# Hybrid decoder step on Trainium2: projections reordered around the score products of the gated recurrence, Pool's products given to ScalarE and VectorE

## The chip, the core and the metric

One NeuronCore of a Trainium2 chip runs the whole program. The metric is the device time of one execution in microseconds (us), median of the runs. The engines are TensorE (PE in the profile; its weight loads are PEld), VectorE (DVE), ScalarE (ACT), GpSimd (POOL) and the sync engine SP, which here only issues transfers.

## What is computed

A single decoder layer for 256 prompt tokens, 16 meta tokens ahead of them and 8 samples of one token each, width 1024, all in float32. From the reference, cut:

```python
u = _rmsnorm(tok, norm_mix[l]) @ w_in[l]          # 7 groups of 512 columns
bg, cg, hv, q, fx, iv, og = jnp.split(u, SPLIT_POINTS, axis=-1)
y_conv = cg * conv3(bg * hv)                      # causal, width 3
f = lb + (1 - lb) * jax.nn.sigmoid(fx); kk = 1 - f
b = jnp.cumsum(log f)                             # per head, 4 heads of 128
scores = einsum('bhtk,bhsk,bhtsk->bhts', q, k, exp(b_t - b_s), causal)
o = scores @ v + (q * jnp.exp(b)) @ S0
S_new = exp(b_last) * S0 + (k * exp(b_last - b)).T @ v
y_rec = per_head_rmsnorm(o) * rec_gain * silu(og)
h = h + concat(y_conv, y_rec) @ w_out
# then: rmsnorm, top-4-of-32 experts (1024 -> 2 x 1024 -> 1024, clamped
# SwiGLU, biases), residual add, final rmsnorm
```

The states of the recurrence and of the convolution are outputs too. The 32 experts' weights are 403 MB of the 431 MB that a run moves.

## The kernel before

**Columns and tiles.** The normalised tokens stand transposed in `xT3` (128 x 8 x 280: 24 columns for samples and meta tokens, then 256 prompt columns). A projection group is 2 MB of weights. Three helpers of the TensorE program use it: `columns_of` (L1280) gives one head's or one quarter's 128 output rows by 280 tokens, eight float32 products; `rows_of` (L1264) gives a tile of 128 tokens by 512 columns, eight products of 512; `stacked` (L1272) does the small tile with 32 narrow products.

**Stage 1** runs forget gate `FX`, value `IV`, query `QG`, output gate `OG`, in this order, each whole, from about 16.5 to 84 us. ScalarE and VectorE make meanwhile from `FX` the gate `f`, its logarithm, the running sums, and the decays, and copy the value and the query out of PSUM.

**Stage 2** is the list `SCHEDULE`, built from `PROJ` (the remaining twelve column groups: `BG` and `HV` by turns, then `CG`) and from `PIECES`, two or three pieces after each group. All engines walk the same list and take from it what is theirs. The pieces: `khat` turns the decayed keys into token rows; `score` is one of 16 score products; `outer` makes the samples' outer products and VectorE adds them to the scaled old states `s0`; `state` and `recur` are the prompt's state and output products, `os` those of the samples.

**Scores.** Each chunk of 128 tokens has a diagonal product and seven levels. For level l the tokens are cut into blocks of 2^l; keys of the earlier block and queries of the later one are scaled by the decay to the border between them. VectorE makes the difference (`diff`, L859), ScalarE two exponentials (`exps`, L611), VectorE the scaled operand (`weigh`, L869), TensorE four products of it with itself (L1342), and VectorE takes from the 128x128 result, by a mask, the part that is this level's (L951). There are two such operands and two PSUM banks (2 and 3) in use by turns, so a product waits for the operand that VectorE made two scores earlier in the list, and for the masked copy before that.

**Pool** makes `vdiag`, the samples' values spread over a diagonal, scales `s0` by the gate (L510, four instructions), and afterwards loads the expert biases and splits them into three bfloat16 parts (L514 to L521).

**Queues.** SP issues the weights in the order of a list and waits for the event that frees each place: the weights and the scratch tiles lie in a ring of eight slots of 2 MB that the expert weights use later. The loads of expert 0 go out one by one in stages 2 and 3: after the output gate, after `HV`, after `CG`, after the samples' states are stored, and in the output projection; a further one then goes out whenever TensorE gives a slot back.

**Stage 3** from 168.6 us: output projection (L1397), router, the choice of the experts, the first gather. **Stage 4** from 219.6 us: 16 pairs of experts, 12 loads of 2 MB a pair. A pair gathers its tokens by one-hot products of bfloat16 parts (L1531, 72 products: 8 column tiles, 3 token tiles, 3 parts), multiplies with the two weight matrices (L1590, L1635), and adds the rows back.

```python
1326                if what == "score":
...
1340                    for h in range(HEADS):
1341                        at = slice(h * P, (h + 1) * P)
1342                        last = mm(ps[:, 2 + a % 2, at], left[:, at], right[:, at], start=True, stop=True)
```

## Time and profile before

| | before |
|---|---|
| median of 3 runs, us | 1161.08 (1159.2 to 1161.52) |
| profiled execution, its own time | 1161.72 |
| span of the profile | 1160.0 |
| TensorE busy | 1062.0 (92%) |
| VectorE, ScalarE, Pool busy | 287.3, 168.3, 48.6 |
| DMA over the span | 431.46 MB, 372 GB/s |
| mean granted clock | 0.987 |
| chain that ended last | PE 61%, DMA 32%, DVE 3%, ACT 2% |

The span is what the trace covers; the profiled execution took 1.7 us more than it, and 0.64 more than the median. Busy shares are averages over four stages; the order of the instructions in time, the waits and the chain that ended last tell what limits each.

### The profile page before, as it was taken

Reading aid. Unit: us, or ns where it says so; the run is one execution under the profiler, and the core shown is the slowest. Engines: PE = TensorE matmul, PEld = TensorE weight load, DVE = VectorE, ACT = ScalarE, POOL = GpSimd, SP = SyncE. Lnnn points to the kernel's source line nnn. Section 1 sums busy time; section 2 is a strip of 40 time slices with the busy share of each in tenths; the row PEclk is TensorE's granted clock in tenths of the full one; section 3 lists DMA queues with packets and bytes.
Section 4 is the critical chain, followed back from the end, with each engine's and each line's share of the span. In section 5 each row is a group of like instructions: output and inputs, shape, how many; then the busy total and the mean of one; then the engine's idle time right before and its main releaser. Section 6 shows DMA issues by size and latency. Waiting matters only on the chain.

```text
span 1160.0 us, 13518 instructions
## 1 busy us (share of the span) xinstructions
PE 1062.0 (92%) x5617; PEld 485.9 (42%) x5617; DVE 287.3 (25%) x513; ACT 168.3 (15%) x381; POOL 48.6 (4%) x71
## 2 busy tenths in 40 slices
PE   6998899899999999899989998999898989898986
PEld 5666764443434343434343434343434343434322
DVE  3447742630202020202020202020202020202023
ACT  3311103310101010101010101010101010101012
POOL 3260012000000000000000000000000000000000
PEclk9999999899999999999999999999999999999998
DMA  9860238399999999999999999999999999999991
GB/s 335 292 241 4 99 147 314 112 409 429 428 425 429 427 429 427 428 430 426 431 427 427 431 426 431 427 428 430 426 431 427 429 429 427 431 425 429 427 429 76
DMA packets 47842, 431.46 MB, mean 372 GB/s; under 512 B 4942, under 2 KB 13686, under 8 KB 23136
## 3 DMA queue, kind: packets, MB, share of 16 engines
q1 hardware_dynamic: 45760, 428.23, 88.4%
q0 software_dynamic: 752, 2.56, 0.7%
q8 instruction: 23, 0.38, 0.1%
q10 hardware_dynamic: 1296, 0.20, 0.1%
q14 instruction: 11, 0.09, 0.0%
HBM read 427.50 MB, written 3.48 MB: 372 GB/s over the span
## 4 chain that ended last, share of the span: by engine, by line
PE 61%; DMA 32%; DVE 3%; ACT 2%; issue 2%; SPq 1%; ACTq 0%; DVEq 0%
DMA ring<-in_expert_w 31%; PE ps L1635 19%; PE ps L1590 17%; PE ps L1286 7%; PE ps L1531 5%; PE ps L1268 2%; PE ps L1397 2%; PE ps L1548 2%; ACT mem L722 2%; PE ps L1624 2%; PE ps L1342 1%; DMA ring<-in_meta_tokens 0%; SPq L387 0%; PE ps L1260 0%; PE ps L1276 0%
## 5 line engine op out<-in xcount | busy, mean ns | idle before, releaser
L1590 PE MATMUL ps<-ring,mem 128*64 128x512 f32 x2048 | 459.2, 596 | 42.4 <-DMA ring<-in_expert_w 41.9
L1590 PEld LDWEIGHTS ps<-ring,mem 128*64 128x64 f32 x2048 | 155.1, 137 | 335.8 <-issue 334.8
L1635 PE MATMUL ps<-ring,mem 128*64 128x512 f32 x1024 | 225.2, 597 | 5.3 <-ACT mem L738 3.0
L1117 DVE TENSOR_TENSOR mem<-mem,ps 128x1024 f32<-128x1024 f32 x32 | 39.1, 1222 | 463.6 <-PE ps L1548 463.6
L1635 PEld LDWEIGHTS ps<-ring,mem 128*64 128x64 f32 x1024 | 86.0, 138 | 133.6 <-issue 133.6
L731 ACT ACTIVATE mem<-mem 128x512 f32<-128x512 f32 x32 | 20.2, 630 | 569.0 <-DVE mem L1179 569.0
L1286 PE MATMUL ps<-mem,ring 128*128 128x280 f32 x320 | 82.7, 417 | 1.0 <-DVE mem L933 0.6
L1548 PE MATMUL ps<-mem 128*128 128x512 f32 (+3 forms) x192 | 80.0, 610 | 0.0
L1286 PEld LDWEIGHTS ps<-mem,ring 128*128 128x128 f32 x320 | 62.6, 200 | 18.7 <-issue 2.8
L1531 PEld LDWEIGHTS ps<-mem 128*128 128x128 bf16 x1080 | 60.3, 98 | 12.2 <-issue 12.2
L1531 PE MATMUL ps<-mem 128*128 128x128 bf16 x1080 | 62.9, 219 | 0.0
L1179 DVE TENSOR_SCALAR mem<-ps 128x512 f32<-128x512 f32 x32 | 22.1, 692 | 146.4 <-PE ps L1590 146.4
L751 ACT ACTIVATE mem<-ps 128x512 f32<-128x512 f32 x32 | 19.1, 597 | 209.2 <-PE ps L1635 209.2
L1548 PEld LDWEIGHTS ps<-mem 128*128 128x128 f32 (+3 forms) x192 | 23.3, 154 | 54.3 <-issue 54.3
L1121 DVE TENSOR_TENSOR mem<-mem,ps 8x512 f32<-8x512 f32 x16 | 10.8, 675 | 118.6 <-PE ps L1548 118.6
L722 ACT ACTIVATE mem<-ps,mem 128x128 f32<-128x128 f32 x124 | 35.3, 368 | 27.2 <-PE ps L1531 24.3
L1624 PE MATMUL ps<-mem 128*128 128x128 f32 x128 | 20.3, 304 | 16.5 <-ACT mem L722 13.7
L1397 PE MATMUL ps<-ring,mem 128*128 128x512 f32 x64 | 28.9, 600 | 0.2 <-DVE mem L933 0.2
L1268 PE MATMUL ps<-ring,mem 128*128 128x512 f32 x64 | 27.8, 592 | 0.0
L1624 PEld LDWEIGHTS ps<-mem 128*128 128x128 f32 x128 | 17.1, 210 | 17.9 <-issue 12.1
L1342 PE MATMUL ps<-ring 128*128 128x128 f32 x112 | 16.6, 300 | 8.2 <-DVE ring L875 8.2
L1181 DVE TENSOR_SCALAR mem<-ps 128x512 f32<-128x512 f32 x32 | 21.8, 681 | 0.0
(268 smaller groups left out, 521.0 us busy)
## 6 DMA issues: line engine op xcount, KB each, us to landing
ring<-in_expert_w SPq DMA_DIRECT2D x192, 2048.0 KB, 26.8
ring<-in_w_in SPq DMA_DIRECT2D x7, 2048.0 KB, 20.6
ring<-in_w_out SPq DMA_DIRECT2D x2, 2048.0 KB, 10.1
ring<-in_state_rec SPq DMA_DIRECT2D x4, 512.0 KB, 10.5
out<-ring SPq DMA_DIRECT2D x4, 512.0 KB, 11.0
out<-mem SPq DMA_DIRECT2D x5, 256.0 KB, 5.2
ring<-in_x_prompt SPq DMA_DIRECT2D x2, 512.0 KB, 4.4
mem<-in_x_prompt POOLq DMA_DIRECT2D x2, 512.0 KB, 4.1
```

The lines of the kernel that those rows point to most:

```text
L722: last = act.activation(xgT4[:, k, 4 * half + q], ps[:, 6 + half, q * P:(q + 1) * P], ACT.Copy, scale=gffn_q[:, 4 * half + q:4 * half + q ...
L1117: dve.tensor_tensor(h3[:, m], h3[:, m], ps[:, 4 + 2 * m:6 + 2 * m, :].rearrange("p a n -> p (a n)"), ALU.add)\
L1179: dve.tensor_scalar(glu[:, at], psA[:, half * D:(half + 1) * D:2], LIMIT, None, ALU.min)\
L1268: last = mm(ps[:, bank, :], xT3[:, t, at:at + P], w_sb[g][:, t, :], start=(t == 0), stop=(t == KT - 1))
L1286: last = mm(ps[:, bank, 0:TOK], w_sb[g][:, t, j * P:(j + 1) * P], xT3[:, t, :], start=(t == 0), stop=(t == KT - 1))
L1342: last = mm(ps[:, 2 + a % 2, at], left[:, at], right[:, at], start=True, stop=True)
L1397: last = mm(ps[:, (6, 4)[i] + n, :], yT3[:, k, TILE_COL[i]:TILE_COL[i] + P], wout_sb[k // 4][:, t, n * 512:(n + 1) * 512], start=(k == 0), ...
L1531: last = mm(out, hn_hi_mid_lo[m][:, part, part_cols(t)], oh5[:, k, m].rearrange("p e s -> p (e s)"), start=(m == 0 and part == 0), stop=(m ...
L1548: last = mm(to, left[:, m * P:m * P + r], right[:, half * HALF:(half + 1) * HALF], start=True, stop=True)
L1590: done = mm(ps[CAP * e:CAP * e + CAP, b, :], xgT4[:, k, t, CAP * e:CAP * e + CAP], ring[:, slot[e], col:col + HALF], start=False, stop=(t ...
L1624: done = pe.transpose(ps[:, 6 + half, q * P:(q + 1) * P], lin[:, half * HALF + q:(half + 1) * HALF:4], ident)
L1635: done = mm(ps[CAP * e:CAP * e + CAP, 4 + half, :], actT3[:, 4 * v + t, CAP * e:CAP * e + CAP], ring[:, slot[e], col:col + HALF], start=(v ...
```

## The change

* **Order of the stages.** Query weights are loaded second, and TensorE projects `FX`, then `QG` (into banks 0, 1, 4, 7 at once, one for each head). `IV` and `OG` move into `SCHEDULE`, in halves of four products of 512 (`rows_of` has a parameter `half`) or as the small stacked tile, with one score product after each. The `BG`, `HV` and `CG` groups follow, also mostly with one score between two groups.
* **Half-width products.** A level's product streams only the later blocks' columns, 64 instead of 128 a head, and the masked copy handles 256 elements instead of 512. The diagonal product stays.
* **Pool's work.** `vdiag` and the scaling of `s0` become eight ScalarE copies with a scale each (five times eight in all); the bias split becomes three ScalarE copies and two VectorE subtractions. Pool asks for the biases after the first forget group. The clearing of `b1_raw` is gone.
* **Gathers.** The sample tile's products use 8 rows instead of 128, in the first gather and in every pair.
* The gate arithmetic (sigmoid times value, L889 to L891) and the scaled queries `qhat` stand in the schedule instead of ahead of it.

```diff
-        PIECES = [("khat", 0)] + [("score", s) for s in range(3)] + [("outer", 0)] + ...
-        PROJ = [(g, j) for j in range(4) for g in (BG, HV)] + [(CG, j) for j in range(4)]
+        Q_BANKS = [0, 1, 4, 7]
+        SCHEDULE = [("rows", (IV, 0, 0))] + DIAG[0] + [("rows", (IV, 0, 1))] + level(0)
+        SCHEDULE += [("rows", (IV, 1, 0)), ("khat", 0)] + level(1) + [("rows", (IV, 1, 1))] + level(2)
+        SCHEDULE += [("b1", 0), ("rows", (IV, 2, 0)), ("vdiag", 0)] + level(3) + [("rows", (OG, 0, 0)), ("s0", 0)] + level(4)
+        SCHEDULE += [("rows", (OG, 0, 1)), ("s0", 1)] + level(5) + [("rows", (OG, 1, 0)), ("s0", 2)] + level(6)
...
+        SCHEDULE += [("proj", (BG, 1)), ("outer", 1), ("proj", (HV, 1))] + level(9)
...
             sp.dma_start(w_sb[FX], w_group(FX)).then_inc(win_in[FX], 16)
+            sp.dma_start(w_sb[QG], w_group(QG)).then_inc(win_in[QG], 16)
             sp.dma_start(w_sb[IV], w_group(IV)).then_inc(win_in[IV], 16)
-            sp.dma_start(w_sb[QG], w_group(QG)).then_inc(win_in[QG], 16)
...
-            for h in range(HEADS):
-                pool.tensor_tensor(s0[:, h], s0[:, h], bcast(fS3[:, h].unsqueeze(2), [P, NS, P]), ALU.mult)\
-                    .then_inc(s0f_sb, 1)
-
+            pool.wait_ge(fx_ps, 1)
             for part in range(3):
                 pool.dma_start(b1_raw[32 * part:32 * part + 32, :], expert_b1[0]).then_inc(b1_in, 16)
...
+                if what == "s0":
+                    act.wait_ge(s0_in, 16 * HEADS)
+                    act.wait_ge(fS_sb, 1)
+                    for b in range(NS):
+                        last = act.activation(s0[:, a, b], s0[:, a, b], ACT.Copy, scale=fS3[:, a, b:b + 1])
+                    last.then_inc(s0f_sb, 1)
...
+                if what == "b1":
+                    dve.wait_ge(b1_step, 4)
+                    dve.tensor_tensor(b1_parts[64:96, :], b1_raw[64:96, :], b1_parts[64:96, :], ALU.subtract)\
+                        .then_inc(b1_sb, 1)
...
+                    else:
+                        pe.wait_ge(sog_sb, bank - 4)
                     columns_of(g, j, bank, done)
...
-                        left = right = wl3[:, n % 2]
+                        left = wl3[:, n % 2]
+                        later = cut(left, 2 << STEPS[n][1])[:, :, 1 << STEPS[n][1]:]
...
+                            last = mm(ps[:, 2 + a % 2, h * 64:(h + 1) * 64], left[:, at],
+                                      later[:, h * m:(h + 1) * m], start=True, stop=True)
...
-                            last = mm(out, hn_hi_mid_lo[m][:, part, part_cols(t)],
-                                      oh5[:, k, m].rearrange("p e s -> p (e s)"),
+                            r = [P, P, NS][m]
+                            last = mm(out, hn_hi_mid_lo[m][0:r, part, part_cols(t)],
+                                      oh5[0:r, k, m].rearrange("p e s -> p (e s)"),
```

**Where the instructions stand.** TensorE before, from the second half of stage 1 into the schedule (L1268 and L1276 are `rows_of` and `stacked`, L1286 `columns_of`, L1323 and L1326 the khat turns, L1342 the score products, L1352 the outer products):

```order
L1286 MATMUL ps<-mem,ring 128x280 x32
L1268 MATMUL ps<-ring,mem 128x512 x16
L1276 MATMUL ps<-ring,mem 32x128 x32
L1286 MATMUL ps<-mem,ring 128x280 x8
L1323 MATMUL ps<-mem 128x128 x8
L1326 MATMUL ps<-mem 128x128
L1342 MATMUL ps<-mem 128x128 x4
L1286 MATMUL ps<-mem,ring 128x280 x8
L1342 MATMUL ps<-ring 128x128 x8
L1352 MATMUL ps<-ring,mem 128x512 x3
L1286 MATMUL ps<-mem,ring 128x280 x8
```

TensorE of the change, behind forget gate and query (L1289, L1298 are now the rows and the stacked tile, L1308 the column groups, L1367 the diagonal score, L1370 a level's score, L1347 and L1349 the khat turns):

```order
L1308 MATMUL ps<-mem,ring 128x280 x64
L1289 MATMUL ps<-ring,mem 128x512 x4
L1367 MATMUL ps<-mem 128x128 x4
L1289 MATMUL ps<-ring,mem 128x512 x4
L1370 MATMUL ps<-ring 128x64 x4
L1289 MATMUL ps<-ring,mem 128x512 x4
L1347 MATMUL ps<-mem 128x128 x8
L1349 MATMUL ps<-mem 128x128
L1370 MATMUL ps<-ring 128x64 x4
L1289 MATMUL ps<-ring,mem 128x512 x4
L1370 MATMUL ps<-ring 128x64 x4
L1298 MATMUL ps<-ring,mem 32x128 x32
```

The scores moved ahead of most of the value and gate rows, which now stand between them; a level's products have 64 columns.

ScalarE of the change, around the fourth to the sixth level (L629 copies the value, L644 is the bias copy, L649 vdiag, L616 the exponentials of the levels, L655 the scaling of `s0`, L635 the gate's exponential):

```order
L616 ACTIVATE ring<-ring 128x16x16 x2
L644 ACTIVATE mem<-mem 32x2048
L629 ACTIVATE mem<-ps 128x128
L649 ACTIVATE ring<-mem 128x128 x8
L616 ACTIVATE ring<-ring 128x8x32 x2
L655 ACTIVATE ring<-ring,mem 128x128 x8
L616 ACTIVATE ring<-ring 128x4x64 x2
L635 ACTIVATE mem<-ps 128x512
L655 ACTIVATE ring<-ring,mem 128x128 x8
L616 ACTIVATE ring<-ring 128x256 x2
```

Groups of eight small products that Pool did in one instruction now stand between the exponentials of the levels.

VectorE of the change, from the bias subtraction to the first gate (L914 the subtraction, L879 `diff`, L888 `weigh`, L972 the masked copy, L909 to L911 the gate):

```order
L914 TENSOR_TENSOR mem<-mem 32x2048
L879 TENSOR_TENSOR ring<-mem 128x512
L888 TENSOR_TENSOR ring<-ring,mem 128x16x16 x2
L972 COPY_PREDICATED ring<-mem,ps 128x32x8
...
L972 COPY_PREDICATED ring<-mem,ps 128x4x64
L909 TENSOR_SCALAR mem<-mem 128x512
L910 RECIPROCAL mem<-mem 128x512
L911 TENSOR_TENSOR mem<-mem,ps 128x512
```

The subtraction stands ahead of a level's preparation, and the gates stand between the masked copies instead of ahead of all scores.

## Rows read from the trace of the kernel before

**Rows 1.** The chain that ended last: start us, us, what.
```profile
253.35 4.14 PE ps L1531 x72
...
275.12 7.02 PE ps L1590 x32
...
329.74 7.02 PE ps L1590 x32
...
939.47 7.09 PE ps L1590 x32
...
998.21 7.09 PE ps L1590 x32
```

**Rows 2.** A window of the expert stage: busy by engine, clock, DMA share, GB/s.
```profile
234.00:239.00 5.00, 5.00 (x23) 1.59 (x23) 1.22 (x1) 0.00 (x0) 0.00 (x0) 1.00 0.99 423
```

**Rows 3.** Timeline of TensorE, stage 1: start us, us, line, instructions.
```profile
33.64 13.90 PE L1268 MATMUL ps<-ring,mem 128*128 128x512 f32 x32
47.46 1.95 PE L1276 MATMUL ps<-ring,mem 128*32 128x128 f32 x64
49.35 15.36 PE L1286 MATMUL ps<-mem,ring 128*128 128x280 f32 x64
64.55 13.90 PE L1268 MATMUL ps<-ring,mem 128*128 128x512 f32 x32
...
80.26 4.04 PE L1286 MATMUL ps<-mem,ring 128*128 128x280 f32 x16
```

**Rows 4.** Timeline of TensorE, stage 2 (two records a float32 product).
```profile
84.13 1.04 PE L1323 MATMUL ps<-mem 128*128 128x128 f32 x8
...
101.55 1.95 PE L1342 MATMUL ps<-ring 128*128 128x128 f32 x16
103.33 3.94 PE L1286 MATMUL ps<-mem,ring 128*128 128x280 f32 x16
...
108.09 1.13 PE L1352 MATMUL ps<-ring,mem 32*128 32x512 f32 x6
...
140.53 3.92 PE L1342 MATMUL ps<-ring 128*128 128x128 f32 x16 [3.10 <-DVE ring L875]
...
155.60 1.94 PE L1380 MATMUL ps<-ring,mem 128*32 128x512 f32 x16
...
168.60 13.97 PE L1397 MATMUL ps<-ring,mem 128*128 128x512 f32 x32 [0.24 <-DVE mem L933]
```

**Rows 5.** Waits (us in total, times, longest), and a window of stage 2.
```profile
PE ps L1342 <- DVE ring L875: 8.2, 4, 3.1
...
142.00:144.00 2.00, 2.00 (x10) 1.91 (x10) 1.65 (x4) 0.40 (x3) 0.00 (x0) 0.50 1.04 442
```

**Rows 6.** Weight loads and products by line: durations in ns, or busy and mean.
```profile
L1342 PEld LDWEIGHTS ps<-ring x112: 186/192/338, 89.8 to 151.5; 128*128 128x128 f32 x112
...
L1276 PEld LDWEIGHTS ps<-ring,mem 128*32 128x32 f32 x128 | 3.4, 110 | 1.5 <-issue 1.5
...
195.47 0.67 PE L1437 MATMUL ps<-mem 8*128 8x8 f32 x8
...
L1531 PE MATMUL ps<-mem x1080: 219/219/230, 253.3 to 1069.1; 128*128 128x128 bf16 x180
```

**Rows 7.** Timeline of ScalarE, then of VectorE.
```profile
41.42 1.11 ACT L607 ACTIVATE mem<-mem 128x1088 f32<-128x1088 f32 x1 [2.59 <-DVE mem L856]
...
218.19 1.14 ACT L722 ACTIVATE mem<-ps,mem 128x128 f32<-128x128 f32 x4 [2.90 <-PE ps L1496]
...
79.57 3.35 DVE L890 RECIPROCAL mem<-mem 128x512 f32<-128x512 f32 x1
...
113.19 0.70 DVE L866 TENSOR_TENSOR ring<-mem 128x512 f32<-128x512 f32 x1
113.79 0.77 DVE L875 TENSOR_TENSOR ring<-ring,mem 128x256 f32<-128x256 f32 x2
114.46 0.73 DVE L951 COPY_PREDICATED ring<-mem,ps 128x512 f32<-128x512 uint32 x1
```

More of the change, by code:

```diff
@@ L643, in _ @@
                     act.activation(ctmp, ps[:, 5, 0:TOK], ACT.Copy).then_inc(bg_sb, 1)
+                if what == "b1":
+                    act.activation(b1_parts[32:64, :], b1_raw[32:64, :], ACT.Copy).then_inc(b1_step, 1)
+                if what == "vdiag":
+                    act.wait_ge(own_sb, 1)
+                    act.wait_ge(v_sb, 3)
+                    for b in range(NS):
+                        last = act.activation(vdiag[:, b * P:(b + 1) * P], vtok3[:, 2, 0:P], ACT.Copy, scale=own[:, b:b + 1])
+                    last.then_inc(vdiag_sb, 1)
+                if what == "s0":
+                    act.wait_ge(s0_in, 16 * HEADS)
+                    act.wait_ge(fS_sb, 1)
+                    for b in range(NS):
+                        last = act.activation(s0[:, a, b], s0[:, a, b], ACT.Copy, scale=fS3[:, a, b:b + 1])
+                    last.then_inc(s0f_sb, 1)
                 if what == "khat":
@@ L899, in _ @@
             dve.wait_ge(q_sb, HEADS)
-            for c in range(2):
-                dve.wait_ge(decay_exp, c + 2)
-                link(dve.tensor_copy(decay_all[:, 4 * c:4 * c + 4],
-                                     qhat3[:, c].rearrange("p (h t) -> p h t", h=HEADS)[:, :, P - 1]))
-                dve.tensor_tensor(qhat3[:, c], qhat3[:, c], qC3[:, c], ALU.mult).then_inc(qhat_sb, 1)
             weigh(0)
             for what, a in SCHEDULE:
+                if what == "gate":
+                    g = sog3[:, a] if a < 2 else sogS
+                    dve.wait_ge(og_exp, a + 1)
+                    link(dve.tensor_scalar(g, g, 1.0, None, ALU.add))
+                    link(dve.reciprocal(g, g))
+                    dve.tensor_tensor(g, g, ps[:, 5 + a, 0:WIDE[a]], ALU.mult).then_inc(sog_sb, 1)
@@ L1262, in _, with rows_of @@
                         last.then_inc(xT_ps, 1)
-            def rows_of(g, i, bank, done):
+            def rows_of(g, i, half, bank, done):
                 at = TILE_COL[i]
-                for t in range(KT):
+                for t in range(4 * half, 4 * half + 4):
                     last = mm(ps[:, bank, :], xT3[:, t, at:at + P], w_sb[g][:, t, :],
                               start=(t == 0), stop=(t == KT - 1))
-                last.then_inc(done, 1)
+                if half:
+                    last.then_inc(done, 1)
             def stacked(g, bank, done):
@@ L1293, in _ @@
                 columns_of(FX, h, 2 + h % 2, fx_ps, first=(h == 0))
-            pe.wait_ge(win_in[IV], 16)
-            for i in range(2):
-                rows_of(IV, i, 5 + i, iv_ps)
-            stacked(IV, 7, iv_ps)
             for h in range(HEADS):
-                if h >= 2:
-                    pe.wait_ge(q_sb, h - 1)
-                columns_of(QG, h, h % 2, q_ps)
-            pe.wait_ge(win_in[OG], 16)
-            pe.wait_ge(fx_exp, HEADS)
-            for i in range(2):
-                rows_of(OG, i, 2 + i, og_ps)
-            stacked(OG, 4, og_ps)
-            pe.wait_ge(v_sb, 3)
-            for what, a in SCHEDULE:
+                columns_of(QG, h, Q_BANKS[h], q_ps)
+            for what, a in SCHEDULE:
+                if what == "rows":
+                    g, i, half = a
+                    if half == 0:
+                        pe.wait_ge(win_in[g], 16)
+                        if g == OG:
+                            pe.wait_ge(v_sb, i + 1)
+                        elif i == 2:
+                            pe.wait_ge(q_sb, HEADS)
+                    done = iv_ps if g == IV else og_ps
+                    if i < 2:
+                        rows_of(g, i, half, 5 + i, done)
+                    else:
+                        stacked(g, 7, done)
                 if what == "proj":
@@ L1329, in _ @@
                     if a < 2:
[L1330 removed]
+                        pe.wait_ge(fx_exp, HEADS)
                     else:
@@ L1495, in gather_first @@
                 for t in steps:
-                    last = mm(ps[:, 6 + t // 4, (t % 4) * P:(t % 4 + 1) * P], hn_hi_mid_lo[m][:, part, part_cols(t)],
-                              oh5[:, 0, m].rearrange("p e s -> p (e s)"), start=(m == 2 and part == 0 and t % 4 == 0),
+                    r = [P, P, NS][m]
+                    last = mm(ps[:, 6 + t // 4, (t % 4) * P:(t % 4 + 1) * P], hn_hi_mid_lo[m][0:r, part, part_cols(t)],
+                              oh5[0:r, 0, m].rearrange("p e s -> p (e s)"), start=(m == 2 and part == 0 and t % 4 == 0),
                               stop=(m == 1 and part == 2 and t % 4 == 3))
```

113 lines of the change are left out of this document (60 added, 53 removed).

## The prediction

> **What bounds the kernel now.** I read the chain that ended last first. The pairs of experts follow each other at a fixed pace there: early in the run the same step comes back after 329.74 - 275.12 = 54.6 us, late in the run after 998.21 - 939.47 = 58.7 us [rows 1]. A late period is twelve loads of 2.1 MB, 25.2 MB in 58.7 us, or 429 GB/s; the window at 234 us, one and a half periods after the expert stage began, already shows the DMA engines 0.99 busy at 423 GB/s [rows 2]. So the early pairs run at TensorE's pace on a ring of eight full slots, the late ones at the transfers' pace, and the transfers are busy without a break from the moment when the first slots are given back. The end is therefore that moment plus a fixed amount of bytes. It moves one for one with the time at which TensorE enters the expert stage, and nothing that is saved inside a pair of experts (4.1 us of slack in each late pair) moves it.
>
> Next I looked at what stands before that stage, on TensorE alone, in order of time. From 33.64 to 80.26 us it has no gap: value rows 13.82 us, the stacked small tile 1.89, four query column groups 64.55 - 49.35 = 15.2 (3.80 each), output gate rows like the value rows [rows 3]. From 80.26 us to the start of the output projection at 168.60 the picture is another: a score of four products takes (103.33 - 101.55)/2 = 0.89 us when nothing is in the way, while two scores together took 3.92 us at 140.53 [rows 4]. The waits view says why: four waits of scores for the scaled operand that VectorE makes (the function weigh), 8.2 us in all, the longest 3.1, and behind the long one the granted clock is 0.50, the lower of its two levels, 1.2 GHz [rows 5].
>
> **What TensorE's work there is without waits.** Twelve column groups of 3.80 = 45.6; sixteen scores of 0.89 = 14.2; the khat turns 1.2 (eight in 1.04, and a ninth); three rounds of outer products of 1.1 = 3.3; the state products, twelve at a score's rate of 0.223 = 2.7; two recur steps, sixteen products each of the same kind over both = 3.6; the sample products 1.9 [rows 3, 4]. Sum 72.5 us. It took until about 167.8 (0.8 before 168.60, in which the small turns stand), that is 87.5 from 80.26. So **15.0 us are lost** there, 8.2 as the waits above, the rest as smaller waits and work at half clock.
>
> **The change, part by part.**
> (1) *Order.* The query moves up behind the forget gate, and its operands are ready at about 33.6 + 15.2 = 48.8 us, where before the scores began at 84. The value and gate rows (31.4 us, now in eight halves of 3.46 and two stacked tiles) and the twelve column groups stand between the scores, one piece of some 3.5 to 7.6 us between two scores. A score's preparation on VectorE is 0.70 + 0.77 + 0.73 = 2.2 us, plus an exponential on ScalarE [rows 7]. It fits into each gap. Before, pairs and triples of scores stood back to back with 0.9 us in between, and that is what could not be covered. If no wait is left, the output projection's start is 33.64 + 46.6 (80.26 - 33.64, same rows and groups) + 72.5 + 0.8 = 153.5 instead of 168.60: **-15.1 us**.
> (2) *Which waits come closest.* I walked the new order with the durations above. ScalarE now has five groups of eight small products (vdiag and four s0), each group 8 x 0.285 = 2.3 us (four 128x128 with a scale in 1.14 [rows 7]), and three bias copies of 2048 columns, about 1.9 to 2.2 each by the 1.11 us for 1088. VectorE has two bias subtractions of 2048 columns, 2.4 each by 0.60 for 512 (113.79 - 113.19), and three gates of which two cost 3.35 for the reciprocal plus 1.1. The subtraction in the schedule ends at about 72.2, the operand for the fifth level (level 4) at 73.5, and TensorE reaches that score at 73.7: slack 0.2. The second gate ends at 95.4, and TensorE wants its bank for the first HV group at 95.3: a tie. Everywhere else the slack is some 0.9 us or more. The bias rows are asked for on Pool's queue after the first forget group, at about 33.6 - 3 x 3.8 = 22.2, and ScalarE wants them before its decay exponential, which ran at 41.42 [rows 7]; were they late, the query copies behind them on ScalarE would be late too. They are 0.8 MB beside full transfers, and the nearest row is only the 2 MB at 423 GB/s, so 2 to 10 us; I take them as in time. For the two ties and the handshakes I take off 0.6: **+0.6**, with 0 and 7.5 (half of today's loss) as ends.
> (3) *Half-width products.* Fourteen level scores stream 64 columns instead of 128, the weights stay 128 columns wide. A score is eight TensorE records, 0.111 each. Does the record get shorter? Its weight load takes 192 ns against 110 ns for 32 columns [rows 6]: 82 ns for 96 columns, 0.85 ns a column, 109 ns for 128. That is the whole record already, so the load bounds it and streaming less saves nothing. The other bound is the shortest record here with 128 weight columns, the 8-row turns at 0.67/8, at most 0.084, and less the tail, 0.59/8 = 0.074 [rows 6]; they are turns, a different kind, and would give 14 x 8 x (0.111 - 0.074) = 4.1 us. Pure streaming at half would give 14 x 8 x 0.055 = 6.2. I take **0**, and keep 6 as the far end. VectorE's masked copy gets shorter (256 columns), which only adds slack.
> By the Trainium skill ("TensorE: Matmul & The Clock Gate", section on LDWEIGHTS) the load time grows with the columns of the weights alone, 128 of them in 107 ns, and its section on the back-to-back issue gap gives a matmul of up to 64 columns some 60 cycles; by the first the sum keeps its 0 here, by the second it would be the 6 us of pure streaming. The measured slope is on the side of the first.
> (4) *Pool relieved.* Its products and bias arithmetic lay beside TensorE's gapless stretch and nothing in the chain waited for them: 0. Covered now by the rows that TensorE does meanwhile; without that cover it is item 2's price.
> (5) *Eight-row gathers.* The sample tile's gather products (24 of 72 a pair) run with 8 rows. Inside the pairs they cannot help (slack above), in the first gather they stand before a wait: 0.
> (6) *Queues.* Each load of SP waits for the same event as before. The first expert load waits for the output gate (80.3 before, 89.5 now, wanted only in the expert stage), the others for the HV and CG groups, the stores, and the output projection, which all move with TensorE. 0. The second output weight waits for the value rows (about 69 now) and is wanted only in the second half of the output projection.
>
> Sum: 15.1 - 0.6 = **14.5 us** less. The profiled execution took 1161.72 us (span 1160.0) and so becomes 1147.2; it lies 0.64 above the median of 1161.08, from which I get **1146.6 us**. About 0.2% (2.3 us) is what a measurement tells from no change.
>
> **Rivals.**
> *The half width pays* (against: the slope of the loads; for: turns with short streams do run at 0.074). 4 to 6 us more: 1140.5 to 1142.5. The skill's section on the issue gap, named above, is the rule that would bring this about.
> *A new wait on ScalarE or VectorE takes the place of the old.* ScalarE is strictly in order: 2.3 us of s0 products stand before an exponential, and the bias arithmetic before the fifth operand. If these forty products took 0.4 instead of 0.285, the ScalarE chain is 4.6 us longer between 70 and 90 us, the gates and exponentials slip, and each wait near 3 us brings a stretch of half clock behind it, as at 140 us. Half of today's loss would remain: 1154. For: two ties; against: all other slacks.
> *The eight-row gathers slow the pairs, and the run ends slower.* Today 72 gathers flow at 4.14/72 = 57 ns [rows 1], though each is 219 ns long by itself [rows 6]. If the change of the row count broke that overlap, 24 x 0.162 = 3.9 us a pair: just under the slack of 4.1, no loss. From 5.1 us a pair on (if the products before and behind are held up too), it costs more than 1 us in each of 15 pairs and cancels the gain; at 6 us it is 15 x 1.9 = 28 - 14.5, so 1175. Nothing in the profile speaks for it but that 128-row and 8-row products never stood side by side here.
> *The change doesn't do what it says*: the expert stage's start is held by something off TensorE, such as the last prefetched loads. Each of them is released by TensorE's own output projection, so I see little for it: 1160 to 1162.
>
> **How the numbers follow.** Forecast (1144 to 1149) 0.62; half width 0.13; new wait, 1150 to 1157, 0.17; gathers 0.04; no effect 0.04. Range: down to the half-width case, 1140.5, up to half of the loss kept, 1154; outside are the worst waits and the last two, some 0.12. Faster by over 0.2%: 0.62 + 0.13 + 0.17 = 0.92; within: 0.04; slower: 0.04.
>
> **What would show it.** In the new profile the output projection starts at 153 to 155; the scores' waits for the scaled operand fall from 8.2 to under 1.5 us; no window from 50 to 150 has a clock of 0.5; level scores still take about 0.89; a late pair takes 58.7 as before, and TensorE waits longer for the ring in all. I am wrong if the start of the output projection moves by 15 and the end doesn't, if scores take 0.5, or if a window between 65 and 100 shows TensorE idle for ScalarE.

## The result, and the profile after

| | before | after |
|---|---|---|
| median of the runs | 1161.3 us (1159.2 to 1161.8, 4 runs) | 1145.94 us (1145.66 to 1146.98, 4 runs) |
| span of the profiled execution | 1160.0 us | 1143.9 us |
| start of the output projection | 168.60 us | 152.07 us |
| first weight product of the experts | 219.57 us | 204.49 us |
| POOL busy | 48.6 us | 23.8 us |

The medians lie 15.4 us apart. The ratio of the runs is 0.9876 with a 95% interval of [0.9862, 0.989], that is 14.4 us less (12.8 to 16.0); the ratio is on record beside the medians and is not their quotient, here and below. The forecast was 1146.6 us. Three executions (1410.77 us in the run of the half width alone, 1424.49 in the bunched one, 2227.62 of the kernel before) were far slower than the rest and stand outside the ratios, but in the counts and medians given; without them those two medians are 1161.48 and 1151.35.

The timeline of TensorE in the kernel after, the answer to [rows 3] and [rows 4] (start us, us, line, instructions, idle time before and its releaser):

```profile
16.34 30.43 PE L1308 MATMUL ps<-mem,ring 128*128 128x280 f32 x128 [0.69 <-ACT mem L584]
46.61 3.60 PE L1289 MATMUL ps<-ring,mem 128*128 128x512 f32 x8
...
54.37 1.00 PE L1370 MATMUL ps<-ring 128*128 128x64 f32 x8
55.21 3.65 PE L1289 MATMUL ps<-ring,mem 128*128 128x512 f32 x8
...
91.99 1.14 PE L1381 MATMUL ps<-ring,mem 32*128 32x512 f32 x6
93.42 4.04 PE L1308 MATMUL ps<-mem,ring 128*128 128x280 f32 x16 [0.29 <-DVE mem L911]
...
152.07 13.11 PE L1428 MATMUL ps<-ring,mem 128*128 128x512 f32 x30 [0.24 <-DVE mem L951]
```

Between 46.61 and 152.07 TensorE has one idle time that shows, 0.29 us: the first HV group waits for the second gate, which is one of the two ties that the prediction named. The scores' waits for the weighed operand, 8.2 us in [rows 5], are gone, and no window of this stretch is below full clock. The stretch takes 105.46 us; the working of the prediction gives 105.3 for it (154.1, its start of the output projection with the 0.6 of item 2, less 48.8). A score takes 54.37 to 55.21, that is 0.84 us.

The pairs, by the chain (start us, us, what), for [rows 1], and the waits (total, times, longest):

```profile
238.28 5.69 PE ps L1564 x72
...
276.02 7.02 PE ps L1623 x32
...
571.78 7.09 PE ps L1623 x32
...
630.53 7.09 PE ps L1623 x32
...
689.27 7.09 PE ps L1623 x32
```

```profile
PE ps L1623 <- DMA ring<-in_expert_w: 13.9, 15, 1.6
```

The late pair takes 58.75 us as before, 4.14 us of gathers have become 5.69, and TensorE's wait for the ring of expert weights (the line above) fell from 41.9 us to 13.9. So something became dearer in the pairs, and it is hidden under the transfers.

### The profile page after: what moved, and what is told of

It reads as the page before. It is cut to its first block, busy times and chain, and to the rows that moved or that the text cites. A ratio compares the mean times of both kernels' runs of the same rounds, so it can differ in the third digit from the quotient of the medians.

```text
span 1143.9 us, 13559 instructions
## 1 busy us (share of the span) xinstructions
PE 1085.4 (95%) x5617; PEld 474.0 (41%) x5617; DVE 288.5 (25%) x515; ACT 185.3 (16%) x424; POOL 23.8 (2%) x60
## 4 chain that ended last, share of the span: by engine, by line
PE 71%; DMA 22%; ACT 2%; DVE 2%; issue 1%; SPq 0%; ACTq 0%; DVEq 0%
PE ps L1623 22%; DMA ring<-in_expert_w 22%; PE ps L1668 20%; PE ps L1564 7%; PE ps L1308 6%; PE ps L1581 3%; PE ps L1289 2%; PE ps L1428 2%; PE ps L1657 2%; ACT mem L735 2%; PE ps L1370 1%; PE ps L1528 1%; PE ps L1573 1%; DMA ring<-in_x_prompt 0%; PE ps L1281 0%
## 5 line engine op out<-in xcount | busy, mean ns | idle before, releaser
L1623 PE MATMUL ps<-ring,mem 128*64 128x512 f32 x2048 | 456.9, 596 | 14.4 <-DMA ring<-in_expert_w 13.9
L1623 PEld LDWEIGHTS ps<-ring,mem 128*64 128x64 f32 x2048 | 145.4, 137 | 313.6 <-issue 312.6
L1668 PE MATMUL ps<-ring,mem 128*64 128x512 f32 x1024 | 232.3, 613 | 4.6 <-ACT mem L751 2.6
L1668 PEld LDWEIGHTS ps<-ring,mem 128*64 128x64 f32 x1024 | 86.0, 141 | 140.4 <-issue 140.4
L1564 PE MATMUL ps<-mem 128*128 128x128 bf16 (+1 forms) x1080 | 86.2, 220 | 0.0
L1308 PE MATMUL ps<-mem,ring 128*128 128x280 f32 x320 | 78.4, 401 | 1.0 <-ACT mem L584 0.7
L1564 PEld LDWEIGHTS ps<-mem 128*128 128x128 bf16 (+1 forms) x1080 | 60.3, 96 | 35.5 <-issue 12.2
L1308 PEld LDWEIGHTS ps<-mem,ring 128*128 128x128 f32 x320 | 59.8, 190 | 17.7 <-issue 3.1
L1581 PEld LDWEIGHTS ps<-mem 128*128 128x128 f32 (+3 forms) x192 | 23.3, 154 | 54.3 <-issue 54.3
L1289 PE MATMUL ps<-ring,mem 128*128 128x512 f32 x64 | 29.1, 597 | 0.0
L1207 DVE SCALAR_TENSOR_TENSOR mem<-mem 128x512 f32<-128x512 f32 x32 | 20.7, 688 | 0.5
```

The source lines that it names most:

```text
L1289: last = mm(ps[:, bank, :], xT3[:, t, at:at + P], w_sb[g][:, t, :], start=(t == 0), stop=(t == KT - 1))
L1308: last = mm(ps[:, bank, 0:TOK], w_sb[g][:, t, j * P:(j + 1) * P], xT3[:, t, :], start=(t == 0), stop=(t == KT - 1))
L1564: last = mm(out, hn_hi_mid_lo[m][0:r, part, part_cols(t)], oh5[0:r, k, m].rearrange("p e s -> p (e s)"), start=(m == 0 and part == 0), sto ...
L1581: last = mm(to, left[:, m * P:m * P + r], right[:, half * HALF:(half + 1) * HALF], start=True, stop=True)
L1623: done = mm(ps[CAP * e:CAP * e + CAP, b, :], xgT4[:, k, t, CAP * e:CAP * e + CAP], ring[:, slot[e], col:col + HALF], start=False, stop=(t ...
L1668: done = mm(ps[CAP * e:CAP * e + CAP, 4 + half, :], actT3[:, 4 * v + t, CAP * e:CAP * e + CAP], ring[:, slot[e], col:col + HALF], start=(v ...
```

## Experiments

The theory by then: the order brings the gain, the work taken off GpSimd nothing, the half width nothing, the eight-row gathers nothing. The first four kernels take the change apart.

**Gathers back to 128 rows, the rest as after.** (`P` in place of `r` in the operands of the gathers, and the padding cleared on GpSimd.)

```diff
-                            r = [P, P, NS][m]
-                            last = mm(out, hn_hi_mid_lo[m][0:r, part, part_cols(t)],
-                                      oh5[0:r, k, m].rearrange("p e s -> p (e s)"),
+                            last = mm(out, hn_hi_mid_lo[m][:, part, part_cols(t)],
+                                      oh5[:, k, m].rearrange("p e s -> p (e s)"),
```

> The changed kernel, but the sample tile's gather products run with all 128 rows again (Pool clears the part of b1_raw behind the samples, as before the change). Theory: the eight-row products cost TensorE 1.55 us a pair (72 gathers took 5.69 instead of 4.14 us), which the transfers hide, and about 1.5 us in the first gather, which nothing hides, since the expert stage began 15.1 us earlier while the output projection began 16.5 us earlier. Then 72 gathers take 4.14 us again, the expert stage begins near 203.0 instead of 204.5, and the run takes about 1144.5 against 1145.9 of the changed kernel. Rival: the longer stretch at half clock in the first gather was chance; then the stage begins at 204.5 and the run takes 1145.9. Second rival: pairs are what bounds the end; then 15 x 1.55 = 23 us less, 1123.

Measured: 1145.66 us (1143.06 to 1147.14, 4 runs), ratio 0.9857 [0.9842, 0.9872]. Gathers 4.14 us, wait for the ring 40.3 us, and 50.95 us from the start of the output projection (153.88) to the first weight product, as the 50.97 of before; the kernel after needs 52.42. So the eight rows cost 1.55 us a pair, hidden, and about 1.5 us in the first gather, which is not hidden but too small to stand out in the whole time. The expert stage itself began at 204.83, not near the 203.0 that was expected, since everything up to the query's end came 1.8 us later in this execution; the section on why the prediction was right comes back to this.

**Scores back to full width, the rest as after.** (The masked copy runs over all columns too.)

```diff
-                        else:
-                            m = later.shape[1] // HEADS
-                            last = mm(ps[:, 2 + a % 2, h * 64:(h + 1) * 64], left[:, at],
-                                      later[:, h * m:(h + 1) * m], start=True, stop=True)
+                        last = mm(ps[:, 2 + a % 2, at], left[:, at], right[:, at], start=True, stop=True)
```

> The changed kernel with level scores of 128 columns a head and the masked copy over 512 elements, as before. Theory (the weight load bounds a short product): a level score goes from 0.84 back to 0.89 us, 14 x 0.05 = 0.7 us, so about 1146.6 against 1145.9. Rival (the stream bounds it): 4 to 6 us more, 1150 to 1152. A second rival: VectorE's longer masked copy uses up the small slacks and TensorE waits for the scaled operand, 1 to 3 us more.

Measured: 1146.93 us (1145.51 to 1148.55, 4 runs), ratio 0.9877 [0.9862, 0.9893]; from the query's end at 46.93 to the output projection at 152.52 it is 105.59 us, beside 105.46. The half width is worth nothing that can be measured here, and 0.13 us of the stretch.

**Eight-row gathers alone, in the kernel before** (the first diff the other way round).

> The kernel before, but the sample tile's gather products run with 8 rows. Theory: 72 gathers take 5.7 us instead of 4.14, an early pair 56.2 instead of 54.6, a late pair 58.7 as before, and the expert stage begins about 1.5 us later than 219.6 if the first gather's longer half clock comes from these products: about 1162.5 against 1161.1. Rival (chance): 1161.1. Rival of the prediction (pairs are held up and the end moves with them): 1184.

Measured: 1162.65 us (1159.67 to 1163.99, 11 runs), ratio 1.0012 [1.0003, 1.0021]. Gathers 5.69 us, early period 56.2 us in place of 54.6, wait for the ring 14.4 us in place of 41.9. One part of the change is a small loss.

**The order alone**: the new table, but full width, 128-row gathers, and GpSimd does the products of vdiag and S0 and the bias split as before. The core of the diff against the kernel before, cut:

```diff
-        PIECES = [("khat", 0)] + [("score", s) for s in range(3)] + [("outer", 0)] + [("score", s) for s in range(3, 6)]
...
+        SCHEDULE = [("rows", (IV, 0, 0))] + DIAG[0] + [("rows", (IV, 0, 1))] + level(0)
...
```

> The changed kernel with only its new order: scores of full width, Pool does vdiag, the scaling of s0 and the bias split, gathers of 128 rows. Theory: the order carries all of the gain; 1145.9 + 0.7 (full width) - 1.5 (first gather) = 1145.1. Rival: ScalarE's and VectorE's taking over of Pool's products carries a part of it, because Pool's results (ready near 80 us) hold the outer products or the scores; then 1147 to 1152. Second rival: half width carries it; then above 1150.

Measured: 1156.25 us (1155.01 to 1156.75, 5 runs), ratio 0.9953 [0.9939, 0.9966]. Here the theory falls: the order alone brings 4.4 us by the medians (1160.61 is the kernel before on that chip), 5.5 by the ratio, of some 15. The first rival names the right part, the work taken off GpSimd, but for another reason and with a smaller loss (1147 to 1152); the second, the half width, is ruled out by the kernel with full-width scores. Its timelines show where the rest went; first TensorE, then VectorE, then GpSimd:

```profile
92.41 1.13 PE L1368 MATMUL ps<-ring,mem 32*128 32x512 f32 x6
103.19 6.00 PE L1301 MATMUL ps<-mem,ring 128*128 128x280 f32 x16 [9.64 <-DVE mem L911]
```

```profile
87.11 3.66 DVE L881 TENSOR_TENSOR ring<-mem 128x512 f32<-128x512 f32 x1
90.69 4.13 DVE L890 TENSOR_TENSOR ring<-ring,mem 128x256 f32<-128x256 f32 x2
94.75 0.71 DVE L965 COPY_PREDICATED ring<-mem,ps 128x512 f32<-128x512 uint32 x1
95.36 3.66 DVE L909 TENSOR_SCALAR mem<-mem 128x512 f32<-128x512 f32 x1
99.05 3.35 DVE L910 RECIPROCAL mem<-mem 128x512 f32<-128x512 f32 x1
```

```profile
86.14 4.08 POOL L525 TENSOR_TENSOR mem<-mem 96x2048 f32<-96x2048 f32 x1
90.28 2.23 POOL L526 CAST mem<-mem 32x2048 bf16<-32x2048 f32 x1
92.56 1.99 POOL L527 CAST mem<-mem 32x2048 bf16<-32x2048 f32 x1
94.63 4.11 POOL L528 TENSOR_TENSOR mem<-mem 32x2048 bf16<-32x2048 f32 x1
```

The two halves of a row of weighing (one row of the profile with x2) take 0.75 us together by themselves and 4.13 here; the add in front of the gate's reciprocal takes 0.42 and here 3.66. The stretched ones end 0.3 to 0.6 us behind an instruction of GpSimd (90.77 against 90.22, 94.82 against 94.55, 99.02 against 98.74), while the masked copy and the reciprocal run at their usual length beside it. The second gate is 9.8 us late (103.13 beside 93.36 in the kernel after), TensorE idles 9.64 us and has a group at half clock behind it (6.00 for 4.04). That is 11.3 us to the output projection (163.80 beside 152.52 of the full-width kernel). In the kernel before, the same GpSimd instructions ran from 49.8 to 80.9 us, where VectorE had little to do. Even there it was not free, though: the profiled execution of the kernel before was only spared by 0.07 us. Its second gate's add began just ahead of GpSimd's last instruction, a clearing (start us, us):

```profile
79.11 0.43 DVE L889 TENSOR_SCALAR mem<-mem 128x512 f32<-128x512 f32 x1 [1.78 <-ACT mem L632]
79.18 1.67 POOL L521 MEMSET mem<- 128x1536 f32 x1
```

```profile
86.45 0.33 PE L1329 MATMUL ps<-mem 128*128 128x128 f32 x1 [1.14 <-DVE mem L891]
```

The last line is from the kernel before with half width, further below. There the add began at 79.25, behind the clearing at 79.18, took 1.59 us, and TensorE waited 1.14 us for the gates. The kernel before with eight-row gathers and the one with doubled gathers, whose instructions are those of the kernel before up to there, show the same (adds of 1.60 and 1.65 us, waits of 1.15 and 1.20). So which of the two begins first, by less than 0.1 us, is worth about 1.2 us in the old order. Where the add came first, the clearing took 1.67 us for 1.38.

New theory: GpSimd's work holds up VectorE's instructions of certain kinds for its whole length, and this costs where VectorE is next on TensorE's path. Four kernels tell which instructions, and whether the spacing of the scores matters beside it.

**GpSimd does vdiag and S0 only.** Added on GpSimd, taken from ScalarE:

```diff
+            pool.tensor_tensor(vdiag.rearrange("p (b v) -> p b v", b=NS),
+                               bcast(vtok3[:, 2, 0:P].unsqueeze(1), [P, NS, P]),
+                               bcast(own.unsqueeze(2), [P, NS, P]), ALU.mult).then_inc(vdiag_sb, 1)
...
+                pool.tensor_tensor(s0[:, h], s0[:, h], bcast(fS3[:, h].unsqueeze(2), [P, NS, P]), ALU.mult)\
+                    .then_inc(s0f_sb, 1)
```

> The kernel after, but GpSimd does the ones products of the values (vdiag) and the scaling of S0 again, as large two-operand instructions; the bias split stays on ScalarE and VectorE. Theory A (what GpSimd's work costs is that VectorE's own instructions stretch while it runs, 0.75 to 4.1 us each, and this reaches TensorE only where VectorE's work is next on TensorE's path): GpSimd's products fall at about 68 to 85 us, so VectorE's weighing and row work there stretches to 3 to 4 us an instruction as in e4, but the stretched scores are only a few us behind other projections: output projection start 152 to 155, time 1145.9 to 1149. Theory B (any two-operand work on GpSimd in the score stage costs as e4 did): output projection start about 160 to 164 and 1154 to 1156.

Measured: 1154.17 us (1152.31 to 1155.73, 6 runs), ratio 0.9949 [0.9932, 0.9967], output projection at 161.00. Time and start are those that theory B named, so the expectation missed. The rows show theory A's mechanism all the same; what failed is its price, since the cover that I had counted on was not there. From the query's end (48.90) to the output projection it is 112.10 us, 6.6 more than in the kernel after. First TensorE, then VectorE, then GpSimd:

```profile
70.05 3.65 PE L1289 MATMUL ps<-ring,mem 128*128 128x512 f32 x8
78.48 1.79 PE L1370 MATMUL ps<-ring 128*128 128x64 f32 x8 [4.77 <-DVE ring L888]
80.06 4.65 PE L1289 MATMUL ps<-ring,mem 128*128 128x512 f32 x8
```

```profile
69.68 2.28 DVE L914 TENSOR_TENSOR mem<-mem 32x2048 bf16<-32x2048 f32 x1 [1.89 <-ACT mem L656]
71.99 2.27 DVE L879 TENSOR_TENSOR ring<-mem 128x512 f32<-128x512 f32 x1
74.19 4.15 DVE L888 TENSOR_TENSOR ring<-ring,mem 128x256 f32<-128x256 f32 x2
```

```profile
70.03 3.69 POOL L514 TENSOR_TENSOR ring<-mem 128x1024 f32<-128x1024 f32 x1 [45.41 <-ACT mem L641]
73.68 8.71 POOL L521 TENSOR_TENSOR ring<-ring,mem 128x1024 f32<-128x1024 f32 x4
```

Here GpSimd is held up as well: its first product takes 3.69 us for 1.90, since VectorE's subtraction, begun 0.35 us before, runs to 71.96. Then each of VectorE's waits for one of GpSimd's (71.99 to 74.26 against 73.72). Whoever begins first keeps the other out for one whole instruction. The bias subtraction stands in front of the fifth level's operand, which was the other tie (in the kernel after that operand is ready at 71.05 and its score begins at 71.25), so TensorE idles 4.77 us.

**GpSimd does the bias split only**, begun when two groups of S0 are scaled.

```diff
+            pool.wait_ge(s0f_sb, 2)
...
+            link(pool.tensor_tensor(b1_raw[0:96, :], b1_raw[0:96, :], b1_parts[0:96, :], ALU.subtract))
...
-            dve.tensor_tensor(b1_raw[0:96, :], b1_raw[0:96, :], b1_parts[0:96, :], ALU.subtract).then_inc(b1_step, 1)
```

> The kernel after, but GpSimd splits the biases again (both subtractions and the copies), begun when two heads' groups of S0 are scaled, about 80 us; the products of vdiag and S0 stay on ScalarE. Theory A (the loss of e4 against the kernel after lies in the GpSimd instructions that run beside VectorE's second gate, at 86 to 99 us): the second gate ends some 5 to 10 us later, TensorE shows an idle stretch of 5 to 9 us ahead of the first state group near 93 us and a window at half clock behind it, output projection start 158 to 163, time 1151 to 1156. Theory B (the loss lay in the earlier products of vdiag and S0, or in the full width): start 152 to 153.5 and the time of the kernel after, 1145 to 1147.

Measured: 1154.11 us (1153.93 to 1155.19, 6 runs), ratio 0.9953 [0.9939, 0.9968], output projection at 160.86. Theory A is right: TensorE idles 6.43 us before the first HV group and that group takes 6.41 for 4.04. From the query's end (46.92) to the output projection it is 113.94 us, 8.5 more than in the kernel after. Which kinds are held up is best seen here, first VectorE, then GpSimd:

```profile
86.65 0.76 DVE L882 TENSOR_TENSOR ring<-mem 128x512 f32<-128x512 f32 x1
87.33 6.31 DVE L891 TENSOR_TENSOR ring<-ring,mem 128x256 f32<-128x256 f32 x2
93.57 0.71 DVE L969 COPY_PREDICATED ring<-mem,ps 128x256 f32<-128x256 uint32 x1
94.08 1.60 DVE L910 TENSOR_SCALAR mem<-mem 128x512 f32<-128x512 f32 x1
95.71 3.35 DVE L911 RECIPROCAL mem<-mem 128x512 f32<-128x512 f32 x1
99.10 0.69 DVE L912 TENSOR_TENSOR mem<-mem,ps 128x512 f32<-128x512 f32 x1
99.71 1.40 DVE L910 TENSOR_SCALAR mem<-mem 128x128 f32<-128x128 f32 x1
```

```profile
86.94 4.39 POOL L514 TENSOR_TENSOR mem<-mem 96x2048 f32<-96x2048 f32 x1
91.40 1.96 POOL L515 CAST mem<-mem 32x2048 bf16<-32x2048 f32 x1
93.40 1.99 POOL L516 CAST mem<-mem 32x2048 bf16<-32x2048 f32 x1
95.48 4.11 POOL L517 TENSOR_TENSOR mem<-mem 32x2048 bf16<-32x2048 f32 x1
99.64 1.38 POOL L518 MEMSET mem<- 128x1536 f32 x1
```

Held up: products with both operands in SBUF (6.31 for 0.75), and the scalar add from SBUF (1.60 for 0.45; the small one 1.40 for 0.22, behind a memset). Not held up: the masked copy and the gate's last product, which read one operand from PSUM, and the reciprocal. By the Trainium skill ("SBUF — State Buffer", section on who interferes with whom) GpSimd and VectorE share one pair of ports that is locked for a whole instruction; a vector instruction with two SBUF inputs contends for it with a GpSimd instruction that reads SBUF, and an operation with a scalar can contend when it runs in a two-port fast mode. These rows agree with it for the kinds that it names, the memset's row too: the add takes 0.42 us for the 512 columns that a product takes 0.68 for, so it may well run in such a mode, which no row shows directly. The reciprocal it does not name.

**The spacing.** The scores of levels 3 to 5 back to back, the rest as after:

```diff
-        SCHEDULE += [("b1", 0), ("rows", (IV, 2, 0)), ("vdiag", 0)] + level(3) + [("rows", (OG, 0, 0)), ("s0", 0)] + level(4)
-        SCHEDULE += [("rows", (OG, 0, 1)), ("s0", 1)] + level(5) + [("rows", (OG, 1, 0)), ("s0", 2)] + level(6)
+        SCHEDULE += [("b1", 0), ("rows", (IV, 2, 0)), ("vdiag", 0), ("rows", (OG, 0, 0)), ("s0", 0)]
+        SCHEDULE += [("rows", (OG, 0, 1)), ("s0", 1)] + level(3) + level(4) + level(5) + [("rows", (OG, 1, 0)), ("s0", 2)] + level(6)
```

> The kernel after, with the score steps of levels 3, 4 and 5 issued back to back behind the projections instead of between them; the work is the same. If the spacing is what removed the waits for the weighed operand: each of the three levels after the first waits for a chain of VectorE and ScalarE of some 4 us less the 3.5 us that the scores' own TensorE work covers, as before (16 waits of 3.9 us in rows of before): TensorE idle 4 to 9 us in all near 85 to 95 us, a window at half clock behind it perhaps, output projection start 156 to 165, time 1150 to 1158. If the spacing does not matter and only the early gate does: start within 1 us of 152 and the time of the kernel after.

Measured: 1151.42 us (lowest 1149.61; 6 runs), ratio 0.992 [0.9903, 0.9937]. One wait came back, with half clock behind it:

```profile
80.43 1.08 PE L1370 MATMUL ps<-ring 128*128 128x64 f32 x8 [2.78 <-DVE ring L888]
81.35 5.35 PE L1289 MATMUL ps<-ring,mem 128*128 128x512 f32 x8
```

2.78 of waiting and 1.70 of slower work (5.35 for 3.65) are 4.5 us for three scores put together; the stretch from the query's end (48.57) to the output projection (158.67) is 4.6 us longer. The idle time is below the 4 to 9 us expected, start and time are as expected. (The "16 waits of 3.9 us" of the expectation is misread: x16 in [rows 4] counts the records of two scores that took 3.92 us together.) The spacing does what item 1 says of it.

**The half width alone, in the kernel before** (the second diff the other way round, and its masked copy).

> The kernel before, with only the score products of the levels cut to the half width (and the masked copies with them). If the weight load bounds such a product (0.84 against 0.89 us a score as seen behind): 24 scores by 0.05 to 0.1 us, most of it inside waits for the weighed operand, so 0 to -1 us: 1159.5 to 1160.6 beside 1160.6. If the columns bound them: 4 x 64 columns fewer at 4 cycles a score, 0.43 us each by 24 = -10 us at most, and with the waits in between still -3 to -10 us.

Measured: 1161.93 us (lowest 1160.49; 12 runs), ratio 1.0013 [1.0, 1.0026]. No gain: a score is 0.05 us shorter (there are fourteen such scores, not the 24 of the expectation), and TensorE is only sooner at the waits for the weighed operand, which stay (2.91, 1.85 and 3.16 us are the longest). The output projection starts at 171.68 in its profile, 3.1 us later than in the one of before: 1.2 of it is the wait for the gate behind GpSimd's clearing, shown above, and most of the rest is longer work at half clock behind the first and the longest wait (a group takes 5.96 us for 5.25, a later one 5.79 for 5.17).

**How much slack the pairs have.** Each gather inside the pairs is done twice, first in the kernel before, then in the one after.

```diff
+                    for again in range(2):
+                        for m in range(3):
```

> The kernel before with each of the 15 gathers inside the pairs done twice (72 more products, 4.14 us a pair; the result is the same). Theory A (the pairs have 4.1 us a pair of slack under the transfers, 54.6 against 58.7 us): the early period becomes 58.7 us, the late one stays 58.7, TensorE's wait for the ring all but goes, time 0 to +3 us: 1160.5 to 1164. Rival (TensorE bounds the pairs): 15 x 4.14 = +62 us, 1223.

Measured: 1172.53 us (1170.83 to 1175.36, 4 runs), ratio 1.0103 [1.0077, 1.0128]. The periods are as expected (254.92 to 313.56 is 58.6), yet it costs 12 us (1160.42 is the kernel before on that chip): 62.1 us were added, so the slack was 50 us in all, 3.3 a pair, not 4.1.

The same edit in the kernel after:

> The kernel after with each gather inside the pairs done twice (5.7 us a pair more). Theory A (slack is now 58.7 - 56.3 = 2.4 us a pair): the period becomes 56.3 + 5.7 = 62.0 us in all 15 pairs against 58.3 on average now, so +45 to +60 us: 1190 to 1206. Rival (the 24 products of 8 rows cost the 1.55 us once, at the change of form, and a second pass costs 4.14): period 60.5, +30 to +38 us: 1176 to 1184.

Measured: 1212.88 us (1211.41 to 1213.03, 4 runs), ratio 1.0445 [1.0426, 1.0465], a doubled gather 11.43 us. That is 67 us more than after for 15 x 5.7 = 86 added: the slack left is 19 us in all, 1.2 a pair. Both expectations were too low. One reason holds for both: the early pairs of the kernels as they are run faster than the transfers, on a ring that was filled ahead, and that lead counts. From first to last gather the period is 57.99 us before (253.30 to 1065.17, 14 periods) and 58.8 with the doubled gathers (254.92 to 1078.17); 14 x 0.81 = 11.4 of the 12.1. In the kernel after there is a second one: with the doubled gathers the period is 62.6 us in the mean (238.65 to 1114.97) and not the 62.0 worked out, which is some 8 us over 14 periods; single ones take up to 63.9 us. Eight windows of 4 us there are below a granted clock of 0.9, which may be the cause; that is not shown.

**What makes the eight-row gathers dear.** Every second column tile begins with its eight-row products, so that there are 8 changes of height in a gather, not 16:

```diff
-                    for m in range(3):
+                    turn = [(0, 1, 2), (2, 0, 1)][t % 2]
+                    for m in turn:
```

> The kernel after, but in the gathers of the pairs every second column tile begins with its 8-row products, so that each run of 8-row products is 6 long instead of 3 and there are half as many changes between 128 and 8 rows (8 instead of 16); the work is the same. If the change between the two heights costs (1.55 us over 16 changes = 97 ns each): a gather takes 4.14 + 0.8 = 4.9 us and the early period 55.4. If each 8-row product costs 65 ns more: it stays 5.7 us and 56.3. The whole time stays within 0.5 us of the kernel after either way, since the pairs have slack: 1145.3 to 1146.5.

Measured: 1146.68 us (1145.24 to 1148.08, 4 runs), ratio 0.9881 [0.986, 0.9902].

```profile
238.40 4.97 PE ps L1565 x72
293.85 4.97 PE ps L1565 x72
```

4.14, 4.97 and 5.69 us for 0, 8 and 16 changes: each change costs about 0.1 us, and the products of eight rows nothing by themselves.

## Why the prediction was right, and where not

The whole: 1146.6 forecast, 1145.94 measured, inside the range, and "faster" came with its chance of 0.92. That it is this near is in part luck. For the profiled execution the forecast was 1147.2 us and it took 1145.66. It gained 2.0 us by chance ahead of the output projection, lost 1.45 in the first gather, which the sum had at 0, and gained 1.0 behind it (939.4 us from the first weight product to the end of the span, 940.4 before), which no run explains.

- **Item 1, the order**: right in its size. The stretch behind the query takes 105.46 us for 105.3 worked out. It ends 2.0 us sooner than forecast (152.07 for 154.1, just outside the "153 to 155" that was to show it) because it begins 2.2 us sooner: gate and query together took 30.43 us, not 32.2. That is the execution's, not the change's. With the same instructions there, five other profiles show 30.43 too and three show 31.98 to 32.36; the forget gate alone took 17.25 us in the kernel before and 15.33 in its variant with eight-row gathers. The difference arises in the first 4 us (6 records against 10 between 18 and 20 us), with the granted clock at 1.00 in both; its cause stays open. So 14.5 of the 16.5 us by which the output projection moved are the change's.
- **Item 2, the ties**: both are real. One shows as 0.29 us of idle time. The other, 0.2 us of slack as worked out, opened as soon as VectorE's work got longer (the kernel with GpSimd's products). The +0.6 held.
- **Item 3, the half width**: right. A score went from 0.89 to 0.84 us, that is 0.105 a record beside the 0.109 worked out for the weight load, and neither kernel that tests it alone shows a gain. Pure streaming would have made it some 0.45 (0.89 less 8 x 0.055).
- **Item 4, "Pool relieved: 0"**: this is the step that failed. It is right in the sum, since item 1's durations for VectorE are those without GpSimd beside it, and wrong as an account. With GpSimd's work left in place the new order gives 4.4 us, not 15, and either half of that work by itself costs some 8 us (1154.17 and 1154.11 beside 1145.94; 6.6 and 8.5 us by the rows). The prediction's "nothing in the chain waited for them" held for the one profile that was read, by 0.07 us; in three variants of the old order TensorE waited 1.14 to 1.20 us at that place. A hint stood in the trace of before: the add in front of the reciprocal took 0.98 us while GpSimd was running and 0.43 at 79.11, between two instructions of GpSimd's. The order alone is not the gain. Taking GpSimd's work away in the old order was not run; an estimate is 1.3 us where GpSimd's clearing begins first (from the end of the forget gate to the output projection 136.28 us in the variant with eight-row gathers, 134.96 in the kernel before), and nothing where it does not.
- **Item 5, eight-row gathers: 0**: the sum's 0 was 1.5 us short. They cost 1.45 us from the output projection to the experts (52.42 for 50.97), and 1.55 in a pair. Over all profiles that stretch takes 51.64 to 52.73 us with eight rows and 50.41 to 51.28 with 128. The rival put the price of a broken overlap at 3.9 us a pair, and the slack at 4.1. Both were too high: 1.55, and 3.3. At 3.9 a pair the kernel would in fact have given away some 9 us of its gain (15 x 0.6), where the rival said none.
- **Item 6, queues: 0**: the experts' first weight product moved by 15.1 us and the end of the span by 16.1.
- **"TensorE waits longer for the ring in all"**: wrong, 13.9 us for 41.9. I had left the gathers unchanged there.
- *A new wait*: none. ScalarE's groups of eight took 2.43 to 2.45 us for the 2.3 worked out, and stood in no one's way.

No version was found that beats the kernel after by more than a measurement tells. The one with 128-row gathers (1145.66) has it equal in time, with 40.3 us of waiting for the ring in hand where it has 13.9.

## What to carry to other kernels

When an order is changed so that an engine's work moves beside another's, read again what each of the two takes with the other running. Durations from a stretch in which VectorE was alone do not hold beside GpSimd, and the cost shows as long vector instructions, not as waits. A single profile can hide it, as the one of before did by 0.07 us. Put an independent piece as long as the operand's preparation between dependent products, and price a broken spacing at the wait plus the half-clock group behind it. And a part that is hidden now (here 1.55 us a pair) still eats the slack that the next change may need.

## What the runs showed of the hardware

- VectorE's instructions with two SBUF operands, and additions of a scalar from SBUF, last until the GpSimd instruction that began before them has ended: 0.68 us became 3.66, 0.75 became 6.31, 0.42 became 3.66. GpSimd is held up in turn, 1.90 to 3.69.
- A change between products of 128 rows and of 8 rows costs TensorE about 0.1 us (4.14, 4.97, 5.69 us for 0, 8, 16 changes).
- Kernels whose gathers use 8 rows show more short stretches at half clock inside the pairs, behind the gather where I looked (302 and 646 us in the kernel after); with 128 rows they are all but absent. In windows of 4 us from 230 to 1030 us, those below 0.9 number 8 after and none before, and 8 in the kernel before with eight-row gathers alone. In the kernel after:

```profile
300.00:302.00 2.00, 1.29 (x10) 0.90 1.06 451
302.00:304.00 2.00, 2.00 (x8) 0.50 0.96 410
304.00:306.00 2.00, 2.00 (x10) 0.75 0.98 418
```

  The number differs between executions of kernels with the same gathers: 3 in the kernel after with full-width scores, 10 in the one with GpSimd's bias split; 1 in the kernel after with 128-row gathers. The down products of the pairs take 613 ns in the mean there, and 597 before (232.3 us busy for 225.2), which adds 7.1 us to the 23.3 that the gathers take more (86.2 for 62.9). It is hidden under the transfers, which stay at their full rate. The first gather shows the same: at half clock from about 193 us, the kernel after is back at 202 to 204 (0.85), the one with 128 rows at 200 to 202 (0.83) though its gather begins 1.8 us later. Why the height of a product bears on it, no run here tells.
